# A three-layer fp32 transformer block on one NeuronCore: in two of its three up projections VectorE alone makes the weights' low part

## The chip, the cores and the metric

The kernel runs on one core of one Trainium2 chip. The metric is the device time of one execution in microseconds (us); the number given for a kernel is the median of several executions. The five engines are written as in the profile: PE is TensorE (matmul), PEld its weight loads, DVE VectorE, ACT ScalarE, POOL GpSimd, and SP the engine that issues the DMAs.

## The reference

Three layers over 272 tokens (16 meta tokens and 256 of input) of width 1024. Cut to the part that matters here, each of the first two layers ends in a feed-forward with a causal convolution over tokens:

```python
def conv_ffn(h, w_up, conv_w, conv_b, w_down):
    L = h.shape[1]
    u = h @ w_up                                   # 1024 -> 2 * 2816
    up = jnp.pad(u, ((0, 0), (CONV_WIDTH - 1, 0), (0, 0)))
    u = conv_b + sum(conv_w[j] * up[:, j:j + L] for j in range(CONV_WIDTH))
    gate, val = jnp.split(u, 2, axis=-1)
    return (jax.nn.silu(gate) * val) @ w_down      # 2816 -> 1024
```

Ahead of it stands an attention mixer (layer 0) or a pooling mixer (layer 1). The third layer has a gated linear attention, a feed-forward without the convolution, and a gate with an embedding projection. Every projection is fed by an RMS norm.

## The kernel before

All data are fp32. TensorE multiplies in fp32r, so every operand is held as a high part (rounded to fp32r) and a low part (what the rounding left), and each product is the sum of three matmuls: high by high, low by high and high by low. They are issued by `three`, lines L383 to L385.

**The weight stream.** The weights come in 121 units (`STREAM`, `UNITS`), in the order in which they are used. An up projection (`up0`, `up1`, `up2`) has 22 units of 16 tiles of 128x128; a unit gives one 128-row block of the gate half and one of the value half. A down projection has 8 units of 22 tiles. Unit n goes through slot n % 2 of three double buffers: `raw` (filled by SP, L320), `w_high` (ScalarE, `high`, L783 and L786) and `w_low` (raw minus high: VectorE, `low`, L1116 and L1121, and GpSimd, its own `low`, L1609). Before the change VectorE makes the low part of the first three quarters of the columns (1536 of the 2048 of an up unit) and GpSimd that of the last quarter (512), which is what `vector_cols` says. In the up loops ScalarE and VectorE work in two pieces: the first is `first_half(n)`, half of VectorE's columns rounded to a tile (768), the second is the rest (1280 for ScalarE, 768 for VectorE). GpSimd waits for all of `high`.

**Who waits for whom.** Semaphores count the units that are done: `high_parts`, `low_parts_v`, `low_parts_g`. TensorE waits at the head of a unit for all three (`parts_ready`, L370 to L372). SP waits for all three of unit n - 2 before it loads unit n into the same slot (`slot_free`, L297 to L299). `high(n)` waits for the load and for the matmuls of unit n - 2.

**A turn of an up loop.** `up_turns` writes the 22 turns of each engine: turns 0, 1, 20 and 21 on their own, and turns 2 to 19 in a hardware loop of two turns a pass. Turn j finishes unit j and prepares the weights of unit j + 2, so turns 20 and 21 prepare the first two units of the down projection. In layers 0 and 1 (`conv` true) VectorE's turn is, in this order, which is fixed since each engine runs its instructions one after the other:

- `scaled` twice (L1173): both blocks out of PSUM, times the norm's row, into `conv_in`. This frees the banks.
- `x_full` (L1219): gate times value of the turn before, after ScalarE's silu.
- `low` in two pieces (L1116, L1121). Turn 0 has none; unit 2 is done before the turns.
- four taps of the convolution (L1248) in place on `conv_out`, after ScalarE's tap (L855).
- `x_low` (L1225): the low part of the product of the turn before.

ScalarE's turn is `high` in two pieces (L783, L786), its tap for both halves (L855), `x_high` of the turn before (L836) and, after VectorE's third tap, silu (L862). GpSimd's turn is one instruction (L1609), from the loop in `up_lows`. The third up projection has no convolution and a shorter turn on VectorE.

The first unit of the down projection reads `x_high` and `x_low` of all 22 turns, chunk by chunk, so its last two chunks wait for the end of turns 20 and 21 and for what follows them.

Stages on the time axis of the trace: attention up to about 185 us, `up0` from about 187, `down0` from 321.6, the pooling mixer, `up1` from about 441, `down1` from 572.4, the third layer's mixer, `up2` from about 788 to 908, then `down2` and the rest.

Of the kernel before, what the change touches and what calls it, by code (L numbers as in the profile page):

```python
# [38 lines left out]
ALU = mybir.AluOpType  # L39
# [95 lines left out]


def vector_cols(n):

    return UNITS[n]["tiles"] * P // 3 if UNITS[n]["name"] == "uqn" else (3 * UNITS[n]["tiles"] // 4) * P

# [29 lines left out]
def program(nc, dram, marks, final):  # L170
    ctx = ExitStack()
    with ctx:
# [115 lines left out]
        def _(sp):  # L288
# [5 lines left out]

            def slot_free(n):

                sp.wait_ge(high_parts, n - 1)  # L297
                sp.wait_ge(low_parts_v, n - 1)
                sp.wait_ge(low_parts_g, n - 1)  # L299

            for name, units, tiles, _, _ in STREAM:
                n0, cols, src = FIRST_UNIT[name], tiles * P, dram["w_" + name]
                if units < 8:
                    for u in range(units):
                        n = n0 + u
                        if n == 0:
                            continue
                        if n >= 2:
                            slot_free(n)
                        sp.dma_start(raw[n % 2][:, 0:cols], src[u, :, :]).then_inc(loaded[n % 2], 16)  # L310
                        if n == 1:
                            for dst, src_ in ((ident[:, :], dram["ident"]), (par[:, DC:NPAR], dram["par"][:, DC:NPAR]),
                                              (rope[:, :, :], dram["rope"]), (cmask[:, :], dram["cmask"])):
                                sp.dma_start(dst, src_).then_inc(tables_in, 16)
                else:
                    with sp.Fori(0, units // 2) as i:
                        for k in range(2):
                            n = 2 * i + (n0 + k)
                            slot_free(n)
                            sp.dma_start(raw[(n0 + k) % 2][:, 0:cols], src[2 * i + k, :, :])\  # L320
# [43 lines left out]
        def _(pe):  # L364
            S = Steps("tensor", step_sems["tensor"], marks)

            def parts_ready(n, i=None):
# [3 lines left out]
                pe.wait_ge(low_parts_v, at)  # L371
                pe.wait_ge(low_parts_g, at)  # L372

# [1228 lines left out]
        def _(pool):  # L1602
            S = Steps("pool", step_sems["pool"], marks)

            def low(n, i=None):
# [3 lines left out]
                nc.gpsimd.tensor_tensor(wl[n % 2][:, at], raw[n % 2][:, at], wh[n % 2][:, at].bitcast(F32),  # L1609
                                        ALU.subtract).then_inc(low_parts_g, 1)  # L1610

# [12 lines left out]
            def up_lows(l):  # L1624
                n0 = FIRST_UNIT[f"up{l}"]
                with pool.Fori(0, (FC - 2) // 2) as i:
                    for k in range(2):
                        low(n0 + k + 2, i)
                for j in range(FC - 2, FC):
# [203 lines left out]
```

## Time and profile before

| what | value |
|---|---|
| median of 3 runs | 1013.43 us (1005.52 to 1014.51) |
| the profiled execution | 1012.96 us |
| its span, first to last instruction | 1011.0 us |
| mean granted TensorE clock | 0.955 of full speed |
| busy, share of the span | PE 92%, PEld 89%, DVE 71%, ACT 50%, POOL 39% |
| largest DVE groups (busy us) | L1121 213.9, L1248 87.1, L1116 64.5 |
| all of L1609 on POOL | 121 instructions, 285.4 us |
| q1, the weights' queue | 144.99 MB, 39.9% of 16 engines |

The profiled execution is 0.47 us below the median of the runs, and 1.96 us of it lie outside the span. Busy shares are averages over stages. The end of a matmul is modelled, so the start-to-start spacing of two matmuls says more than the busy time, and the same holds for two neighbouring instructions on VectorE, whose spans overlap by some 0.08 us. A row of the timeline that ends in "x2" or "x4" is two or four instructions merged, with the time from the first start to the last end. "[0.52 <-PE bank L385]" behind a row is the idle time ahead of it and what ended it; a row without it followed at once.

### The profile page before, as it was taken

The numbers are of one execution on the slowest core, as the hardware profiler recorded it, in microseconds if no ns is written. First come the engines' busy times: TensorE is split into PE (matmuls) and PEld (weight loads), VectorE is DVE, ScalarE is ACT, GpSimd is POOL, SyncE is SP. The second block draws the span as 40 slices with busy tenths as digits, with TensorE's granted clock in tenths as the row PEclk, the third lists the DMA queues.
The fourth block names the chain that finished last, engine by engine and source line by source line (L and its number), as shares of the span: only waits on it lengthen the run. The fifth ranks groups of instructions, "written<-read, shape, count | busy, mean of one in ns | idle before, by whom it ended". The sixth has DMA issues, their size and how long they took to land.

```text
span 1011.0 us, 20095 instructions
## 1 busy us (share of the span) xinstructions
PE 934.1 (92%) x7256; PEld 898.8 (89%) x7256; DVE 718.0 (71%) x1224; ACT 504.3 (50%) x833; POOL 397.0 (39%) x274
## 2 busy tenths in 40 slices
PE   6789987999999997899999899899989999999995
PEld 6687777999999897799999899798989999999994
DVE  7656624899999325389999932679868788885666
ACT  5465634555556434555555533453346445454342
POOL 4434736322223455332222356531216333335633
PEclk9799979899999998989999999899999999999997
DMA  7322013244445453024444545334215545455431
GB/s 261 121 84 84 2 42 130 87 168 166 165 165 207 171 192 125 1 88 171 174 172 175 188 165 198 125 124 180 106 52 187 192 173 198 175 210 212 161 125 42
DMA packets 20848, 145.64 MB, mean 144 GB/s; under 512 B 2480, under 2 KB 4032, under 8 KB 5440
## 3 DMA queue, kind: packets, MB, share of 16 engines
q1 hardware_dynamic: 20800, 144.99, 39.9%
q8 instruction: 31, 0.51, 0.2%
q14 instruction: 17, 0.14, 0.0%
HBM read 143.94 MB, written 1.05 MB: 143 GB/s over the span
## 4 chain that ended last, share of the span: by engine, by line
PE 35%; DVE 9%; ACT 5%; issue 5%; ACTq 1%; DVEq 0%; POOL 0%; POOLq 0%
PE bank L383 11%; PE bank L384 10%; PE bank L385 10%; DVE conv_out L1248 3%; ACT w_high L786 2%; DVE w_low L1121 1%; ACT conv_out L855 1%; ACT w_high L783 1%; PE bank L674 1%; PE bank L447 0%; PE bank L702 0%; DVE conv_out L1589 0%; DVE gla_s_diag L1463 0%; PE bank L703 0%; PE bank L704 0%
## 5 line engine op out<-in xcount | busy, mean ns | idle before, releaser
L1609 POOL TENSOR_TENSOR w_low<-raw,w_high 128x512 fp32r<-128x512 f32 (+1 forms) x121 | 285.4, 2359 | 504.7 <-ACT w_high L786 488.5
L383 PE MATMUL bank<-u_high,w_high 128*128 128x256 f32 (+2 forms) x1472 | 432.8, 294 | 30.9 <-DVE u_low L1130 18.8
L384 PE MATMUL bank<-u_low,w_high 128*128 128x256 f32 (+2 forms) x1472 | 425.0, 289 | 0.0
L385 PE MATMUL bank<-u_high,w_low 128*128 128x256 f32 (+2 forms) x1472 | 424.1, 288 | 0.0
L383 PEld LDWEIGHTS bank<-u_high,w_high 128*128 128x128 f32 x1472 | 285.5, 194 | 42.5 <-issue 23.2
L1121 DVE TENSOR_TENSOR w_low<-raw,w_high 128x768 fp32r<-128x768 f32 (+4 forms) x120 | 213.9, 1782 | 142.3 <-ACT w_high L786 141.0
L384 PEld LDWEIGHTS bank<-u_low,w_high 128*128 128x128 f32 x1472 | 285.4, 194 | 0.0
L385 PEld LDWEIGHTS bank<-u_high,w_low 128*128 128x128 f32 x1472 | 284.9, 194 | 0.0
L786 ACT ACTIVATE w_high<-raw 128x1280 fp32r<-128x1280 f32 (+4 forms) x120 | 206.6, 1722 | 70.2 <-PE bank L385 63.8
L383 PE MATMUL bank<-x_high,w_high 128*128 128x256 f32 (+1 forms) x608 | 174.2, 287 | 10.2 <-DVE x_low L1225 4.8
L385 PE MATMUL bank<-x_high,w_low 128*128 128x256 f32 (+1 forms) x608 | 173.7, 286 | 0.0
L384 PE MATMUL bank<-x_low,w_high 128*128 128x256 f32 (+1 forms) x608 | 173.1, 285 | 0.0
L383 PEld LDWEIGHTS bank<-x_high,w_high 128*128 128x128 f32 x608 | 116.0, 191 | 11.6 <-ACT conv_out L862 3.5
L384 PEld LDWEIGHTS bank<-x_low,w_high 128*128 128x128 f32 x608 | 116.0, 191 | 0.0
L385 PEld LDWEIGHTS bank<-x_high,w_low 128*128 128x128 f32 x608 | 115.7, 190 | 0.0
L1622 POOL TENSOR_TENSOR acc<-acc,sq 128x272 f32<-128x272 f32 (+2 forms) x84 | 68.1, 810 | 76.4 <-ACT sq L802 65.1
L1248 DVE SCALAR_TENSOR_TENSOR conv_out<-conv_in,par,conv_out 128x272 f32<-128x272 f32 (+1 forms) x176 | 87.1, 534 | 6.2 <-ACT conv_out L855 0.7
L783 ACT ACTIVATE w_high<-raw 128x768 fp32r<-128x768 f32 (+1 forms) x66 | 56.7, 859 | 60.5 <-PE bank L385 59.8
L862 ACT ACTIVATE conv_out<-conv_out 128x272 f32<-128x272 f32 (+1 forms) x44 | 18.7, 425 | 110.7 <-DVE conv_out L1248 110.7
L1116 DVE TENSOR_TENSOR w_low<-raw,w_high 128x768 fp32r<-128x768 f32 (+1 forms) x66 | 64.5, 977 | 8.6 <-ACT w_high L783 8.6
L1173 DVE TENSOR_TENSOR conv_in<-bank,r_rows 128x256 f32<-128x256 f32 (+2 forms) x140 | 54.1, 427 | 15.7 <-PE bank L385 10.3
L1130 DVE SCALAR_TENSOR_TENSOR u_low<-h,par,u_high 128x272 fp32r<-128x272 f32 (+3 forms) x56 | 53.1, 966 | 0.9 <-ACT u_high L810 0.9
(182 smaller groups left out, 933.3 us busy)
## 6 DMA issues: line engine op xcount, KB each, us to landing
raw<-w_up_dram SPq DMA_DIRECT2D x66, 1024.0 KB, 4.7
raw<-w_down_dram SPq DMA_DIRECT2D x24, 1408.0 KB, 6.0
raw<-w_gin_c_dram SPq DMA_DIRECT2D x4, 1536.0 KB, 7.7
raw<-w_wo_dram SPq DMA_DIRECT2D x4, 1024.0 KB, 4.7
raw<-w_wout_dram SPq DMA_DIRECT2D x4, 1024.0 KB, 4.7
raw<-w_pgate_dram SPq DMA_DIRECT2D x4, 1024.0 KB, 4.8
raw<-w_gin_v_dram SPq DMA_DIRECT2D x2, 1024.0 KB, 4.7
raw<-w_gin_g_dram SPq DMA_DIRECT2D x2, 1024.0 KB, 5.0
```

What stands on the lines that cost most here:

```text
L383: nc.tensor.matmul(out, hi, rhi, start=start, stop=False)
L384: nc.tensor.matmul(out, hi, rlo, start=False, stop=False)
L385: return nc.tensor.matmul(out, lo, rhi, start=False, stop=stop)
L783: nc.scalar.activation(wh[n % 2][:, 0:split], raw[n % 2][:, 0:split], ACT.Copy).then_inc(*S.step(first))
L786: nc.scalar.activation(wh[n % 2][:, split:cols], raw[n % 2][:, split:cols], ACT.Copy).then_inc(high_parts, 1)
L1116: nc.vector.tensor_tensor(wl[n % 2][:, 0:split], raw[n % 2][:, 0:split], wh[n % 2][:, 0:split].bitcast(F32), ALU.subtract).then_inc(*S.step())
L1121: nc.vector.tensor_tensor(wl[n % 2][:, split:cols], raw[n % 2][:, split:cols], wh[n % 2][:, split:cols].bitcast(F32), ALU.subtract).then_i ...
L1130: nc.vector.scalar_tensor_tensor(ul[:, c, 0:T], h[:, c, t0:t0 + T], pcol(gain, c), uh[:, c, 0:T].bitcast(F32), ALU.mult, ALU.subtract)\
L1173: nc.vector.tensor_tensor(out, bank[BLOCKS[b]["bank"]][:, 0:T], rows[:, 0:T], ALU.mult)\
L1248: nc.vector.scalar_tensor_tensor(cv[:, hf, 0:T], ur[:, hf, skip + tap:skip + tap + T], pcol(f"cw{l}", (tap * 2 + hf) * FC + j), cv[:, hf, ...
L1609: nc.gpsimd.tensor_tensor(wl[n % 2][:, at], raw[n % 2][:, at], wh[n % 2][:, at].bitcast(F32), ALU.subtract).then_inc(low_parts_g, 1)
L1622: nc.gpsimd.tensor_tensor(acc[:, a, 0:T], acc[:, a, 0:T], sq[:, label % 2, 0:T], ALU.add).then_inc(*step)
```

## The change

Units 2 to 21 of `up0` and of `up1` (`pool_share` false) are no longer shared: `vector_cols` is all 2048 columns for them, so VectorE makes the whole low part, in pieces of 1024 and 1024. As `first_half` follows, ScalarE's two pieces become 1024 and 1024 too. GpSimd has no instruction for these 40 units; its next `low` (the first unit of `down0` or `down1`) adds 21 to `low_parts_g` in place of 1, so that the counts agree behind it (`pool_counts`). TensorE leaves out its wait for `low_parts_g` at the head of these units, and SP leaves it out where the unit before in the slot was such a unit; for that four units of `up0` and `up1` and two units of each down projection are written out ahead of SP's loops. Units 0 and 1 of `up0` and `up1`, all of `up2`, and all other units are as before, and so are the results: the same subtraction is done by another engine.

```diff
--- before.py
+++ after.py
@@ -134,8 +134,23 @@
     _x["before"] = next((j for j in range(_i - 1, -1, -1) if BLOCKS[j]["bank"] == _x["bank"]), None)
 
 
+def pool_share(n):
+
+    return UNITS[n]["name"] not in ("up0", "up1") or UNITS[n]["u"] < 2
+
+
+def pool_counts(n):
+
+    first = n
+    while first > 0 and not pool_share(first - 1):
+        first -= 1
+    return n - first + 1
+
+
 def vector_cols(n):
 
+    if not pool_share(n):
+        return UNITS[n]["tiles"] * P
     return UNITS[n]["tiles"] * P // 3 if UNITS[n]["name"] == "uqn" else (3 * UNITS[n]["tiles"] // 4) * P
 
 
@@ -292,11 +307,13 @@
                 sp.dma_start(raw[0][:, cols], dram["w_dq"][0, :, cols])\
                     .then_inc(loaded[0] if p == PIECES - 1 else pieces_in[p], 16)
 
-            def slot_free(n):
+            def slot_free(n, shared=True):
+
 
                 sp.wait_ge(high_parts, n - 1)
                 sp.wait_ge(low_parts_v, n - 1)
-                sp.wait_ge(low_parts_g, n - 1)
+                if shared:
+                    sp.wait_ge(low_parts_g, n - 1)
 
             for name, units, tiles, _, _ in STREAM:
                 n0, cols, src = FIRST_UNIT[name], tiles * P, dram["w_" + name]
@@ -306,17 +323,22 @@
                         if n == 0:
                             continue
                         if n >= 2:
-                            slot_free(n)
+                            slot_free(n, pool_share(n - 2))
                         sp.dma_start(raw[n % 2][:, 0:cols], src[u, :, :]).then_inc(loaded[n % 2], 16)
                         if n == 1:
                             for dst, src_ in ((ident[:, :], dram["ident"]), (par[:, DC:NPAR], dram["par"][:, DC:NPAR]),
                                               (rope[:, :, :], dram["rope"]), (cmask[:, :], dram["cmask"])):
                                 sp.dma_start(dst, src_).then_inc(tables_in, 16)
                 else:
-                    with sp.Fori(0, units // 2) as i:
-                        for k in range(2):
+
+                    apart = 2 if units == DC else 4 if not pool_share(n0 + 2) else 0
+                    for u in range(apart):
+                        slot_free(n0 + u, pool_share(n0 + u - 2))
+                        sp.dma_start(raw[(n0 + u) % 2][:, 0:cols], src[u, :, :]).then_inc(loaded[(n0 + u) % 2], 16)
+                    with sp.Fori(0, (units - apart) // 2) as i:
+                        for k in range(apart, apart + 2):
                             n = 2 * i + (n0 + k)
-                            slot_free(n)
+                            slot_free(n, pool_share(n0 + k - 2))
                             sp.dma_start(raw[(n0 + k) % 2][:, 0:cols], src[2 * i + k, :, :])\
                                 .then_inc(loaded[(n0 + k) % 2], 16)
                 if name == "down0":
@@ -369,7 +391,8 @@
                 at = n + 1 if i is None else 2 * i + (n + 1)
                 pe.wait_ge(high_parts, at)
                 pe.wait_ge(low_parts_v, at)
-                pe.wait_ge(low_parts_g, at)
+                if pool_share(n):
+                    pe.wait_ge(low_parts_g, at)
 
             def bank_free(b, i=None, stride=0):
 
@@ -1607,7 +1630,7 @@
                 at = slice(vector_cols(n), UNITS[n]["tiles"] * P)
                 pool.wait_ge(high_parts, n + 1 if i is None else 2 * i + (n + 1))
                 nc.gpsimd.tensor_tensor(wl[n % 2][:, at], raw[n % 2][:, at], wh[n % 2][:, at].bitcast(F32),
-                                        ALU.subtract).then_inc(low_parts_g, 1)
+                                        ALU.subtract).then_inc(low_parts_g, pool_counts(n))
 
             def clear(after, T=T1):
 
@@ -1623,9 +1646,10 @@
 
             def up_lows(l):
                 n0 = FIRST_UNIT[f"up{l}"]
-                with pool.Fori(0, (FC - 2) // 2) as i:
-                    for k in range(2):
-                        low(n0 + k + 2, i)
+                if pool_share(n0 + 2):
+                    with pool.Fori(0, (FC - 2) // 2) as i:
+                        for k in range(2):
+                            low(n0 + k + 2, i)
                 for j in range(FC - 2, FC):
                     low(n0 + j + 2)
```

## Rows read from the trace of the kernel before

**Rows 1.** The page: busy us of each engine (part 1), chain by line (part 4).

```profile
PE 934.1 (92%) x7256; PEld 898.8 (89%) x7256; DVE 718.0 (71%) x1224; ACT 504.3 (50%) x833; POOL 397.0 (39%) x274
...
PE bank L383 11%; PE bank L384 10%; PE bank L385 10%; DVE conv_out L1248 3%; ACT w_high L786 2%; DVE w_low L1121 1%; ACT conv_out L855 1%; ACT w_high L783 1%; PE bank L674 1%; PE bank L447 0%; PE bank L702 0%; DVE conv_out L1589 0%; DVE gla_s_diag L1463 0%; PE bank L703 0%; PE bank L704 0%
```

**Rows 2.** Windows: length, busy us of PE, PEld, DVE, ACT, POOL; granted clock; DMA share; GB/s.

```profile
250.00:260.00 10.00, 9.85 (x77) 9.42 (x76) 9.45 (x19) 5.32 (x9) 1.54 (x1) 1.00 0.45 156
500.00:510.00 10.00, 9.72 (x79) 9.32 (x78) 9.57 (x15) 5.32 (x10) 2.91 (x2) 1.00 0.37 141
583.00:585.00 2.00, 2.00 (x10) 2.00 (x11) 0.00 (x0) 1.09 (x3) 0.55 (x1) 0.50 0.79 327
```

**Rows 3.** VectorE's timeline, one turn of the first up loop: start us, us, what.

```profile
252.95 0.79 DVE L1173 TENSOR_TENSOR conv_in<-bank,r_rows 128x272 f32<-128x272 f32 x2
253.65 0.43 DVE L1219 TENSOR_TENSOR x_full<-conv_out 128x272 f32<-128x272 f32 x1
254.00 0.95 DVE L1116 TENSOR_TENSOR w_low<-raw,w_high 128x768 fp32r<-128x768 f32 x1
254.87 2.04 DVE L1121 TENSOR_TENSOR w_low<-raw,w_high 128x768 fp32r<-128x768 f32 x1
256.84 1.96 DVE L1248 SCALAR_TENSOR_TENSOR conv_out<-conv_in,par,conv_out 128x272 f32<-128x272 f32 x4
258.71 0.43 DVE L1225 TENSOR_TENSOR x_low<-x_full,x_high 128x272 f32 x1
259.27 0.79 DVE L1173 TENSOR_TENSOR conv_in<-bank,r_rows 128x272 f32<-128x272 f32 x2
```

**Rows 4.** GpSimd's timeline, the same turn and one of the third up loop.

```profile
254.56 1.54 POOL L1609 TENSOR_TENSOR w_low<-raw,w_high 128x512 fp32r<-128x512 f32 x1 [4.80 <-ACT w_high L786]
...
825.40 2.06 POOL L1609 TENSOR_TENSOR w_low<-raw,w_high 128x512 fp32r<-128x512 f32 x1 [3.55 <-ACT w_high L786]
```

**Rows 5.** VectorE's timeline, the same turn of the third up loop.

```profile
825.36 0.96 DVE L1121 TENSOR_TENSOR w_low<-raw,w_high 128x768 fp32r<-128x768 f32 x1
826.23 1.51 DVE L1225 TENSOR_TENSOR x_low<-x_full,x_high 128x256 f32 x1
```

**Rows 6.** Groups by line and shape, 315 to 332 us: count, busy us, mean ns.

```profile
L1121 DVE TENSOR_TENSOR w_low<-raw,w_high 128x1024 fp32r<-128x1024 f32 x2 | 2.5, 1226 | 0.0
L1116 DVE TENSOR_TENSOR w_low<-raw,w_high 128x1024 fp32r<-128x1024 f32 x2 | 2.4, 1218 | 0.0
```

**Rows 7.** TensorE's timeline: unit starts of the first up loop, then L383 at 330.78.

```profile
194.52 0.29 PE L383 MATMUL bank<-u_high,w_high 128*128 128x272 f32 x1
...
200.52 0.29 PE L383 MATMUL bank<-u_high,w_high 128*128 128x272 f32 x1
...
257.21 0.39 PE L383 MATMUL bank<-u_high,w_high 128*128 128x272 f32 x1
...
314.26 0.39 PE L383 MATMUL bank<-u_high,w_high 128*128 128x272 f32 x1
...
330.78 0.36 PE L383 MATMUL bank<-x_high,w_high 128*128 128x272 f32 x1 [1.43 <-DVE x_low L1225]
```

**Rows 8.** TensorE's timeline, second up loop: unit starts, and 453.16 inside the first.

```profile
447.72 0.28 PE L383 MATMUL bank<-u_high,w_high 128*128 128x258 f32 x1
...
453.16 0.28 PE L383 MATMUL bank<-u_high,w_high 128*128 128x258 f32 x1
...
509.26 0.39 PE L383 MATMUL bank<-u_high,w_high 128*128 128x258 f32 x1 [0.16 <-issue]
...
565.14 0.38 PE L383 MATMUL bank<-u_high,w_high 128*128 128x258 f32 x1
```

**Rows 9.** VectorE's timeline: start of turn 20 in the first and second up loops.

```profile
316.25 0.79 DVE L1173 TENSOR_TENSOR conv_in<-bank,r_rows 128x272 f32<-128x272 f32 x2
...
567.05 0.76 DVE L1173 TENSOR_TENSOR conv_in<-bank,r_rows 128x258 f32<-128x258 f32 x2
```

**Rows 10.** ScalarE's timeline, the turn of rows 3.

```profile
254.39 1.10 ACT L855 ACTIVATE conv_out<-conv_in,par 128x272 f32<-128x272 f32 x2
```

## The prediction

> **What bounds the kernel now.** I read four views, from the whole to one turn. The page first [rows 1]: VectorE is busy for 71% of the span, and the chain by line is mostly TensorE's three matmul lines with a few per cent of VectorE's taps and of ScalarE's high part. That is an average over stages, so the stage has to be read by itself. The windows of the two up loops [rows 2] show something else there: VectorE is busy for 9.45 and 9.57 us in 10, at full granted clock, and TensorE for 9.85 and 9.72. VectorE is full, and TensorE has small holes.
>
> The timeline of TensorE says how large they are. In the first up loop a unit of 48 matmuls took 200.52 - 194.52 = 6.00 us at the start, with nothing between the two unit heads. Later the heads stand at 257.21 and 314.26, nine units apart: 6.34 us each [rows 7]. In the second loop (258 tokens wide in place of 272) 15 chunks of three matmuls took 453.16 - 447.72 = 5.44 us, so 16 of them, a unit, take 5.80. From 509.26 to 565.14 nine units took 6.21 each [rows 8]. So TensorE loses 0.34 us a unit in one loop and 0.41 in the other.
>
> Who makes it wait stands in VectorE's timeline [rows 3]. One turn runs from 252.95 to 259.27, 6.32 us, and no row has an idle time: VectorE is the bound of the loop. Start to start, its steps take 0.70 (conv_in), 0.35 (x_full), 0.87 (first low piece), 1.97 (second low piece), 1.87 (taps) and 0.56 us (x_low and the way to the next turn). The second low piece ends at 254.87 + 2.04 = 256.91 and TensorE's next unit starts at 257.21: this is the wait that ends last at the head of a unit.
>
> The two low pieces have the same shape, 128x768, and cost 0.95 and 2.04 us. What differs is that GpSimd's instruction started 0.31 us ahead of the second one [rows 4]. The third up loop is the control: there GpSimd started at 825.40, just after VectorE's second piece at 825.36. That piece took 0.96, and the next VectorE instruction, x_low, took 1.51, where x_low takes 0.43 in the turn of the first loop [rows 3 to 5]. So 1.1 us of VectorE's time is lost once per unit, in whichever two-input instruction meets GpSimd's, and it does not belong to the low piece.
>
> The Trainium skill has this in SBUF — State Buffer, section "Who interferes with whom": a VectorE instruction with two inputs in SBUF and a GpSimd instruction that reads SBUF exclude each other, and the one that came first keeps the port. By that rule, the trace agrees in who waits; the length lost, 2.04 - 0.95, is less than GpSimd's whole 1.54, which is also how the rows overlap.
>
> **The change, part by part.** VectorE's low part. For 40 units the pieces grow from 768 to 1024 columns. That shape is in the trace, in turns 20 and 21: 1.22 and 1.23 us [rows 6], against 0.95. Start to start that is the duration less the usual overlap of 0.08, so about 1.15 each, 2.30 together, where rows 3 have 0.87 + 1.97 = 2.84. Two larger pieces add 2 x 0.27 = 0.54, the lost 1.09 goes, and VectorE's turn gets 0.54 shorter: 6.32 - 0.54 = 5.78 us in the first loop and 6.21 - 0.54 = 5.67 in the second. Both are below TensorE's 6.00 and 5.80, so TensorE becomes the bound, and of the 0.54 only 0.34 and 0.41 count.
>
> ScalarE. Its pieces of 768 and 1280 become 1024 and 1024. The sum of columns is the same. The first piece comes some 0.2 us later (1.04 in place of 0.84), the second ends at the same time. In the turn of rows 3 ScalarE's taps ended at 254.39 + 1.10 = 255.49 [rows 10] and VectorE's taps began at 256.84, so ScalarE is 1.35 us ahead; with VectorE 0.54 faster it stays ahead. I price it at nothing inside the loop. When VectorE has caught up with TensorE, its first piece will wait some 0.1 to 0.3 us for ScalarE's first piece, an estimate. The cover is the 0.13 to 0.22 us between VectorE's turn and TensorE's unit; where that is gone, TensorE still isn't late, since it needs the low part only a whole unit later (5.8 us against about 3.6).
>
> GpSimd, the waits and the loads. GpSimd's 40 instructions go, and nothing else is queued in its loop. TensorE has one wait fewer per unit, SP likewise, and SP's load is released by VectorE's second piece, which now ends sooner. Issues and sizes are the same, only some are written out ahead of the loop. Nothing.
>
> The start of each loop. Unit 2's low part is made ahead of turn 0, without GpSimd beside it, so VectorE pays 0.54 there and again in turn 1. The 1.1 us lost to GpSimd in turn 1 goes at the same time, so VectorE enters turn 2 about where it did. What TensorE could wait there is at most the 0.54 us by which the first banks come free later, once a loop. I take zero, since TensorE's unit 2 follows unit 1 without a hole now, and keep 0.5 for the range.
>
> Units 2 to 21. In the first loop the head of unit 2 is at 194.52, and 19 units later the head of unit 21 would be at 194.52 + 19 x 6.00 = 308.52, where it is 314.26 now [rows 7]: 5.7 us. In the second 447.72 + 19 x 5.80 = 557.92 against 565.14 [rows 8]: 7.2 us. Together 12.9.
>
> The end of each loop is not TensorE's. At 330.78 it waits for x_low of VectorE's turn 20 [rows 7], and once more for turn 21. Turns 20 and 21 keep GpSimd's share and their length, so this end moves with the start of VectorE's turn 20. Now that start is at 316.25 and 567.05, which is 1.99 and 1.91 us behind the head of unit 21 [rows 7 to 9], since VectorE is late all through the loop. With TensorE as the bound VectorE makes up 0.22 us a turn in the first loop, 4.0 us over 18 turns, and in the second 0.13 a turn, 2.3 us; both are more than the 2.0 and 1.9. So turn 20 starts close behind unit 20's end, and I take 0.1 to 0.2: 308.6 and 558.1. The ends move by 316.25 - 308.6 = 7.65 and 567.05 - 558.1 = 8.95. From each I take 0.15 for the first low piece of turn 20, which now waits a little for ScalarE: 7.5 + 8.8 = 16.3 us. Behind it the down projection runs on TensorE's time, so the gain is kept.
>
> Sum against the profiled execution: 1012.96 - 16.3 = 996.7. The median of the runs is 0.47 above that execution, hence 997.
>
> One term I can't place: TensorE's clock. Behind the two waits at the end of the second loop it fell to half (0.50 from 583 to 585 [rows 2]), 1.3 us or so lost over 2.7 us. The new waits there will be some 0.3 us shorter in sum. The fall may go, or one may come behind the first loop, where there is none now: 1.3 either way.
>
> **The rivals.** The tail gives nothing. If VectorE doesn't catch up (its turn is 5.9 rather than 5.7, by waits that are now hidden), only the 12.9 us of TensorE's unit heads are won: 1000.5. For it: in the second loop the margin is only 0.13 us a turn. Against: no idle row in VectorE's turn [rows 3].
>
> ScalarE's chain is the bound. The chain of the page has its high part and VectorE's taps in it [rows 1], which reads like a circle silu, high, tap, taps. If it set the turn, VectorE's shorter low part would only become idle time, and the time would stay at 1013. Against: the 1.35 us between ScalarE's tap and VectorE's [rows 3, 10], which VectorE's second low piece fills.
>
> Slower: the 1.1 us is a cost of the second piece itself (it runs beside ScalarE's taps), not of GpSimd. Then the new second piece takes 1.22 + 1.10 = 2.32, the two pieces some 3.38 start to start, and a turn grows by 0.54: 40 turns, +21.6 us, 1034. It decides from the point where the two pieces take more than today's 2.84. Against: the piece of 0.96 in rows 5, and the two of rows 6. The Trainium skill, Perfetto Trace Analysis, section "Optimizing Scalar/DVE Operations", speaks on both sides: with VectorE saturated some of its work may be worth giving to another engine, GpSimd included, but between these two it might not help, for their common port. The first half of that is what the change undoes; the trace agrees with the second half, by the 1.1 us lost against the 0.54 that the columns cost.
>
> **How the numbers follow.** 997 has 0.70, with a range of its own from 993 to 1000 (the clock 1.3 either way, the start 0.5, 0.05 us a turn on 40 turns for TensorE's rate, 2). The tail giving nothing has 0.13, ScalarE's chain 0.09 and the slower case 0.05; 0.03 is for what I don't see. The three runs of before lie 9 us apart, so a median can fall some 4 us beside the profile. To hold 8 in 10 I take 989 to 1004: the first case with that spread, and the second one. Faster by over 1% (below 1003.3; 1% is about what a measurement of this kernel can tell from no change) is the first two cases less the spread: 0.79. Within 1%: 0.15. Slower by over 1%: 0.06.
>
> **What would show it.** In the changed profile both low pieces should be 1.22 us at 128x1024 in all 40 turns. TensorE's unit heads should stand 6.00 and 5.80 us apart without a hole. VectorE should have short idle times in late turns that end at TensorE or at ScalarE's first high piece. Turn 20 should start near 308.6, and in the second loop near 550.6 (558.1 less the first loop's 7.5). GpSimd should be empty in the loops. A second piece above 1.3 us, or unit heads further apart than 6.05 and 5.85, would prove me wrong.

## The result, and the profile after

| kernel | median of its runs | beside it, before |
|---|---|---|
| changed | 994.67 us (992.07 to 996.30, 4 runs) | 1010.70 us (1005.52 to 1014.51, 4 runs) |
| changed, a second set | 994.65 us (991.24 to 996.17, 5 runs) | 1011.39 us (1009.33 to 1013.54, 9 runs) |

The ratio to the kernel before is 0.9838, 95% interval 0.9807 to 0.9868, and in the second set 0.9835, 0.9811 to 0.9858. The profiled executions took 1012.96 and 996.30 us, 16.66 less; 16.3 was predicted, and 997 for the median. That the median came out 2.3 us below 997 has little to do with the change: the prediction started from a median of 1013.43 us for the kernel before (3 runs), and beside the changed kernel it is 1010.70, which less 16.3 is 994.4.

Line numbers of the changed kernel are 23 higher in the part shown: L383 to L385 are L406 to L408, L1116 and L1121 are L1139 and L1144, L1609 is L1632.

The windows of the changed kernel, with the columns of [rows 2] and at the same times (the third is one window of 2 us behind the second loop's end):

```profile
250.00:260.00 10.00, 10.00 (x82) 10.00 (x81) 9.32 (x16) 6.35 (x11) 0.00 (x0) 1.00 0.42 151
500.00:510.00 10.00, 10.00 (x85) 10.00 (x85) 9.45 (x17) 6.44 (x11) 0.00 (x0) 1.00 0.47 168
568.00:570.00 2.00, 2.00 (x17) 2.00 (x18) 0.00 (x0) 1.32 (x3) 0.74 (x1) 1.00 0.84 349
```

TensorE is busy for 10.00 us in 10, where it was 9.85 and 9.72. VectorE is a little under its old value, and GpSimd is empty. TensorE's granted clock behind the second loop is 1.00, the upper of its two levels (2.4 GHz), where it was 0.50, the lower one (1.2 GHz).

VectorE's timeline of the changed kernel, one turn late in the first loop:

```profile
285.07 0.79 DVE L1196 TENSOR_TENSOR conv_in<-bank,r_rows 128x272 f32<-128x272 f32 x2
285.78 0.43 DVE L1242 TENSOR_TENSOR x_full<-conv_out 128x272 f32<-128x272 f32 x1
286.33 1.23 DVE L1139 TENSOR_TENSOR w_low<-raw,w_high 128x1024 fp32r<-128x1024 f32 x1
287.48 1.22 DVE L1144 TENSOR_TENSOR w_low<-raw,w_high 128x1024 fp32r<-128x1024 f32 x1
288.62 1.97 DVE L1271 SCALAR_TENSOR_TENSOR conv_out<-conv_in,par,conv_out 128x272 f32<-128x272 f32 x4
290.50 0.43 DVE L1248 TENSOR_TENSOR x_low<-x_full,x_high 128x272 f32 x1
291.06 0.79 DVE L1196 TENSOR_TENSOR conv_in<-bank,r_rows 128x272 f32<-128x272 f32 x2
```

ScalarE's timeline of the changed kernel, its first high piece of the same turn:

```profile
285.24 1.06 ACT L806 ACTIVATE w_high<-raw 128x1024 fp32r<-128x1024 f32 x1 [0.60 <-PE bank L408]
```

Against [rows 3]: the pieces cost 1.23 and 1.22 us in place of 0.95 and 2.04, and all 88 pieces of this shape in the two stages took 1.22 or 1.23. The turn is 5.99 us long, TensorE's length, and a first slack shows: 0.55 us from x_full to the first low piece, where it was 0.35. VectorE waits there for ScalarE, whose high piece ends at 286.30, and ScalarE waited for TensorE (the 0.60 in its row). This is the order of a loop that TensorE bounds.

TensorE's timeline of the changed kernel: head of unit 2 and of unit 21 of the second loop, then the first matmul of chunk 20 in layer 0's first down unit:

```profile
441.22 0.28 PE L406 MATMUL bank<-u_high,w_high 128*128 128x258 f32 x1
...
551.42 0.28 PE L406 MATMUL bank<-u_high,w_high 128*128 128x258 f32 x1
...
324.29 0.37 PE L406 MATMUL bank<-x_high,w_high 128*128 128x272 f32 x1 [1.32 <-DVE x_low L1248]
```

(551.42 - 441.22) / 19 = 5.80 us a unit, where [rows 8] have 6.21. In the first loop the heads of units 2 and 21 stand at 195.04 and 309.04, 19 units of 6.00 us apart, and no matmul of either loop between these heads has an idle time ahead of it.

**Where the 16.7 us went.** Two marks bound each loop's stage: the matmul in the middle of unit 1 that waits for the norm's rows, and the first matmul of chunk 21 in the first down unit, which waits for VectorE's turn 21. All stage lengths below are differences of two such starts on TensorE's timeline.

| stage, us | before | changed | difference |
|---|---|---|---|
| start to first mark | 191.42 | 191.94 | +0.52 |
| first loop and tail | 140.85 | 133.83 | -7.02 |
| between the loops | 112.47 | 112.47 | 0.00 |
| second loop and tail | 138.13 | 129.73 | -8.40 |
| chunk 21 of down1 to the next norm's matmul at 639.74 and 623.33 | 56.87 | 55.36 | -1.51 |

The loops give 15.4 us. The 1.5 us behind the second loop is the clock: it was at half from 583 to 585 and in part up to 587, and now isn't. The other profiles bear this out: the stretch of the last row takes 56.70 to 56.88 us in the four that have this fall (before, e1, e3, e9) and 55.21 to 55.42 in the eight that don't. The rest of the kernel is as it was to within 0.1 us. The sum is 7.0 + 8.4 + 1.5 + 0.1 - 0.5 = 16.5 us of the span; the other 0.2 of the 16.66 lie outside the span.

These stage lengths are much sharper than whole times. The mark in unit 1 of the first loop stood between 186.33 and 191.94 us in the profiles of this study. Nothing that the kernels change lies ahead of it but a memset of GpSimd's at the start of e8 and e9 and, in the norm just before it, GpSimd's low part of unit 2. The granted clock differs there: 0.87 from 20 to 60 us and 0.91 from 60 to 100 in the kernel before, 0.83 and 1.00 in e5. That is not the whole of it, for e3 had the clock of before up to 100 us, a lower one behind it (0.84 against 0.86 from 100 to 186), and its mark all the same 0.84 us earlier. Behind that mark stages that should be equal agree to 0.02 us. So the experiments are read by their stages, and by their medians only where those are far apart.

### The profile page after: what moved, and what is told of

It reads as the page before. It is cut to its first block, busy times and chain, and to the rows that moved or that the text cites. A ratio compares the mean times of both kernels' runs of the same rounds, so it can differ in the third digit from the quotient of the medians.

```text
span 994.5 us, 19919 instructions
## 1 busy us (share of the span) xinstructions
PE 923.7 (93%) x7256; PEld 895.8 (90%) x7256; DVE 698.3 (70%) x1224; ACT 506.6 (51%) x833; POOL 335.0 (34%) x234
## 3 DMA queue, kind: packets, MB, share of 16 engines
HBM read 143.94 MB, written 1.05 MB: 146 GB/s over the span
## 4 chain that ended last, share of the span: by engine, by line
PE 78%; DVE 12%; ACT 5%; issue 2%; POOL 1%; DMA 1%; SPq 0%; POOLq 0%; DVEq 0%; ACTq 0%
PE bank L406 22%; PE bank L407 22%; PE bank L408 22%; DVE w_low L1144 2%; PE bank L580 2%; ACT w_high L809 2%; PE bank L566 2%; DVE conv_out L1271 1%; PE bank L697 1%; PE bank L596 1%; DVE u_low L1153 1%; PE bank L667 1%; PE bank L470 1%; PE bank L455 1%; PE bank L460 1%
## 5 line engine op out<-in xcount | busy, mean ns | idle before, releaser
L406 PE MATMUL bank<-u_high,w_high 128*128 128x256 f32 (+2 forms) x1472 | 429.1, 292 | 27.1 <-DVE u_low L1153 17.9
L408 PE MATMUL bank<-u_high,w_low 128*128 128x256 f32 (+2 forms) x1472 | 424.2, 288 | 0.0
L1632 POOL TENSOR_TENSOR w_low<-raw,w_high 128x512 fp32r<-128x512 f32 (+1 forms) x81 | 223.8, 2764 | 551.4 <-ACT w_high L809 535.1
L406 PEld LDWEIGHTS bank<-u_high,w_high 128*128 128x128 f32 x1472 | 286.1, 194 | 31.4 <-issue 13.0
L1144 DVE TENSOR_TENSOR w_low<-raw,w_high 128x1024 fp32r<-128x1024 f32 (+4 forms) x120 | 186.0, 1550 | 142.3 <-ACT w_high L809 141.1
L408 PEld LDWEIGHTS bank<-u_high,w_low 128*128 128x128 f32 x1472 | 285.3, 194 | 0.0
L809 ACT ACTIVATE w_high<-raw 128x1024 fp32r<-128x1024 f32 (+5 forms) x120 | 197.9, 1650 | 70.3 <-PE bank L408 63.7
L406 PE MATMUL bank<-x_high,w_high 128*128 128x256 f32 (+1 forms) x608 | 173.5, 285 | 7.9 <-DVE x_low L1248 4.7
L408 PE MATMUL bank<-x_high,w_low 128*128 128x256 f32 (+1 forms) x608 | 173.0, 285 | 0.0
L406 PEld LDWEIGHTS bank<-x_high,w_high 128*128 128x128 f32 x608 | 115.2, 190 | 9.3 <-ACT conv_out L885 3.3
L408 PEld LDWEIGHTS bank<-x_high,w_low 128*128 128x128 f32 x608 | 115.0, 189 | 0.0
L806 ACT ACTIVATE w_high<-raw 128x1024 fp32r<-128x1024 f32 (+1 forms) x66 | 65.7, 995 | 77.6 <-PE bank L408 77.5
L1139 DVE TENSOR_TENSOR w_low<-raw,w_high 128x1024 fp32r<-128x1024 f32 (+1 forms) x66 | 75.5, 1143 | 11.9 <-ACT w_high L806 9.1
L825 ACT ACTIVATE sq<-bank 128x272 f32<-128x272 f32 (+1 forms) x24 | 9.4, 394 | 86.8 <-PE bank L408 86.8
```

The lines of the kernel that those rows point to most:

```text
L406: nc.tensor.matmul(out, hi, rhi, start=start, stop=False)
L408: return nc.tensor.matmul(out, lo, rhi, start=False, stop=stop)
L806: nc.scalar.activation(wh[n % 2][:, 0:split], raw[n % 2][:, 0:split], ACT.Copy).then_inc(*S.step(first))
L809: nc.scalar.activation(wh[n % 2][:, split:cols], raw[n % 2][:, split:cols], ACT.Copy).then_inc(high_parts, 1)
L1139: nc.vector.tensor_tensor(wl[n % 2][:, 0:split], raw[n % 2][:, 0:split], wh[n % 2][:, 0:split].bitcast(F32), ALU.subtract).then_inc(*S.step())
L1144: nc.vector.tensor_tensor(wl[n % 2][:, split:cols], raw[n % 2][:, split:cols], wh[n % 2][:, split:cols].bitcast(F32), ALU.subtract).then_i ...
```

## The experiments

Each is told as an edit of the changed kernel unless it says otherwise.

**e1: GpSimd reads, and nobody waits for it.**

```diff
+        scratch = sb("scratch", [P, 512])
...
                 if pool_share(n0 + 2):
                     ...
+                else:
+                    for j in range(FC - 2):
+                        pool.wait_ge(high_parts, n0 + j + 3)
+                        pool.wait_ge(*S.now())
+                        nc.gpsimd.tensor_tensor(scratch[:, 0:NPAR], par[:, 0:NPAR], par[:, 0:NPAR],
+                                                ALU.subtract).then_inc(*S.step())
```

> The changed kernel, and beside it GpSimd subtracts a table of 476 columns from itself into a scratch tile once in each of the 40 turns, at the moment where its low part ran before (after ScalarE's high part); nobody waits for it. Theory (GpSimd's instruction that reads SBUF holds up VectorE's instruction with two inputs): VectorE loses about 1.0 us a turn (476 of 512 columns of 1.1), its turn goes from 5.78 and 5.67 to 6.8 and 6.7 us and is the bound again; TensorE's unit heads stand 6.8 and 6.7 apart in place of 6.00 and 5.80; some +32 to +36 us, 1027 to 1031. Rival (the 1.1 us belonged to VectorE's second low piece, or to the wait for the low part): nobody waits for the added work, so 995 as the changed kernel.

Measured: 1019.76 us (1018.58 to 1021.44, 4 runs), ratio to before 1.009 (1.006 to 1.0121), 25 us above the changed kernel. By stages 145.20 and 142.58, that is +11.4 and +12.9. VectorE's timeline of e1, and GpSimd's instruction:

```profile
251.06 0.79 DVE L1197 TENSOR_TENSOR conv_in<-bank,r_rows 128x272 f32<-128x272 f32 x2
251.76 0.43 DVE L1243 TENSOR_TENSOR x_full<-conv_out 128x272 f32<-128x272 f32 x1
252.11 1.22 DVE L1140 TENSOR_TENSOR w_low<-raw,w_high 128x1024 fp32r<-128x1024 f32 x1
253.25 2.00 DVE L1145 TENSOR_TENSOR w_low<-raw,w_high 128x1024 fp32r<-128x1024 f32 x1
...
257.60 0.79 DVE L1197 TENSOR_TENSOR conv_in<-bank,r_rows 128x272 f32<-128x272 f32 x2
...
252.66 1.50 POOL L1658 TENSOR_TENSOR scratch<-par 128x476 f32<-128x476 f32 x1 [5.07 <-ACT w_high L810]
```

The mechanism is shown: an instruction whose result nobody reads brings the slow second piece back, and with it a turn of 6.54 us in place of 5.99. The rival (995) falls. The size was short of what I expected, 0.78 us lost in place of 1.0, and a turn of 6.54 in place of 6.8; e8 takes that up. The total holds some 3 us that are not the turns': in e1 the granted clock fell to 0.50 behind both loops (from 333 to 336 us and from 589 to 592), which made the stretches behind them 1.8 and 1.3 us longer than in the changed kernel.

**e2: GpSimd only writes.** As e1, with the instruction replaced:

```diff
-  nc.gpsimd.tensor_tensor(scratch[:, 0:NPAR], par[:, 0:NPAR], par[:, 0:NPAR], ALU.subtract)
+  nc.gpsimd.memset(scratch[:, 0:512], 0.0)
```

> As e1, but GpSimd's added instruction only writes: a memset of 512 columns (272 columns took 0.33 us in the profile, so this takes some 0.5). Theory (what is shared is the way by which GpSimd reads): no change, 995, VectorE's pieces stay at 1.22 us. Rival (any GpSimd instruction holds VectorE up for its length): 0.5 us a turn, VectorE's turn 6.3 and 6.2, +12 to +16 us, about 1009.

Measured: 991.89 us (991.43 to 993.44, 4 runs), ratio 0.9815 (0.9787 to 0.9844); stages 133.83 and 129.72, the changed kernel's to 0.01 us.

VectorE's second piece in the timeline of e2, and GpSimd's memset of the same turn:

```profile
252.77 1.22 DVE L1145 TENSOR_TENSOR w_low<-raw,w_high 128x1024 fp32r<-128x1024 f32 x1
...
252.59 0.53 POOL L1658 MEMSET scratch<- 128x512 f32 x1 [5.47 <-ACT w_high L810]
```

The memset runs across the start of the second piece, as the reading instruction did, and the piece keeps its 1.22 us. The rival (1009) falls. So it is not GpSimd's being busy, and not its writing, but its reading. The Trainium skill says just this in SBUF — State Buffer, section "Who interferes with whom": a VectorE instruction with two SBUF inputs contends with a GpSimd instruction that reads SBUF and not with one that only writes. By that rule, e1 and e2 agree.

**e8: two tables in place of one twice.** As e1, with a second table of the same width that GpSimd fills at the start:

```diff
-  nc.gpsimd.tensor_tensor(scratch[:, 0:NPAR], par[:, 0:NPAR], par[:, 0:NPAR], ALU.subtract)
+  nc.gpsimd.tensor_tensor(scratch[:, 0:NPAR], par[:, 0:NPAR], table2[:, 0:NPAR], ALU.subtract)
```

> As e1, but GpSimd's added subtraction reads two different tables of 476 columns in place of one table twice. In e1 VectorE's second piece lost 0.78 us (2.00 in place of 1.22), where 512 columns of the real low part cost 1.09. If reading one table twice is what made e1 cheap, the loss is 1.0 and VectorE's turn 6.8 us in the first loop; if it is where GpSimd begins in VectorE's turn (0.59 us ahead of the second piece in e1, 0.31 in the kernel before), it is 0.78 and 6.54 again.

One run: 1022.90 us. The timeline of e8, the same instructions as in e1:

```profile
252.44 0.79 DVE L1198 TENSOR_TENSOR conv_in<-bank,r_rows 128x272 f32<-128x272 f32 x2
...
253.50 1.22 DVE L1141 TENSOR_TENSOR w_low<-raw,w_high 128x1024 fp32r<-128x1024 f32 x1
254.63 2.23 DVE L1146 TENSOR_TENSOR w_low<-raw,w_high 128x1024 fp32r<-128x1024 f32 x1
...
254.06 1.73 POOL L1659 TENSOR_TENSOR scratch<-par,table 128x476 f32<-128x476 f32 x1 [5.08 <-ACT w_high L811]
```

The second piece took 2.23 to 2.25 us over the turns, a loss of 1.02 on average, and the turn 6.78 (from 252.44 to 259.22). The stages are 149.96 and 147.33, +33.7 us on the changed kernel in sum, inside what e1 had been expected to cost; the whole time is less far up, since the first mark stands 5.6 us earlier than in the changed kernel's first profile. GpSimd begins 0.57 us ahead of the second piece, as in e1 (0.59), so its place in the turn is not the reason. A subtraction of one table from itself holds VectorE up for less than one of two tables, 0.78 against 1.02 us at the same 476 columns. Why, no run here shows.

**e9: one input.** As e8, with

```diff
+  nc.gpsimd.tensor_scalar(scratch[:, 0:512], table2[:, 0:512], 1.5, None, ALU.mult)
```

> As e1, but GpSimd's added instruction is a tensor_scalar of 512 columns with one SBUF input. Theory (every GpSimd instruction that reads SBUF keeps VectorE's two-input instruction waiting, for about as long as it runs beside it): VectorE loses 0.4 to 1.0 us a turn. Rival (only GpSimd's two-input instructions do): nothing, VectorE's pieces stay at 1.22 and the unit heads at 6.00 us.

One run: 1003.95 us; stages 137.86 and 135.23, +4.0 and +5.5.

The timeline of e9, VectorE's two pieces and GpSimd's instruction of the same turn:

```profile
254.26 1.22 DVE L1141 TENSOR_TENSOR w_low<-raw,w_high 128x1024 fp32r<-128x1024 f32 x1
255.40 1.63 DVE L1146 TENSOR_TENSOR w_low<-raw,w_high 128x1024 fp32r<-128x1024 f32 x1
...
254.77 2.06 POOL L1659 TENSOR_SCALAR scratch<-table 128x512 f32<-128x512 f32 x1 [4.12 <-ACT w_high L811]
```

It loses VectorE 0.41 us, at the low end of the expectation, and the rival (nothing) falls. GpSimd's record is 2.06 us long and runs for 1.43 us beside VectorE's second piece, which still loses only 0.41. So the theory's "for about as long as it runs beside it" fails for an instruction with one input.

**e7: GpSimd's share doubled, on the kernel before.**

```diff
 def vector_cols(n):
 
+    if UNITS[n]["name"] in ("up0", "up1") and UNITS[n]["u"] >= 2:
+        return 8 * P
```

> The kernel before with GpSimd's share of the 40 units raised from 512 to 1024 columns; VectorE's pieces fall to 512 and 512. Theory (VectorE loses time in proportion to GpSimd's columns): the loss goes from 1.1 to about 2.2 us and VectorE wins 0.54, so its turn grows by 0.56 us, 6.9 and 6.8; about +22 us on the kernel before, 1032. Rival (the loss is a fixed 1.1 us for each instruction that meets): VectorE's turn falls by 0.54 to 5.8 and 5.7, TensorE is the bound, 995.

Measured: 1031.92 us (1030.66 to 1037.24, 4 runs), ratio 1.0222 (1.019 to 1.0253); stages 151.59 and 149.15, +21.8 us in sum on the kernel before.

The timeline of e7, the same three instructions:

```profile
255.24 0.68 DVE L1118 TENSOR_TENSOR w_low<-raw,w_high 128x512 fp32r<-128x512 f32 x1
255.84 2.90 DVE L1123 TENSOR_TENSOR w_low<-raw,w_high 128x512 fp32r<-128x512 f32 x1
...
255.80 2.40 POOL L1611 TENSOR_TENSOR w_low<-raw,w_high 128x1024 fp32r<-128x1024 f32 x1 [4.54 <-ACT w_high L788]
```

Two pieces of the same 512 columns, 0.68 and 2.90 us: 2.22 lost for 1024 of GpSimd's columns, 1.09 for 512 before. That is 2.1 to 2.2 ns a column, and VectorE does a column itself in (1.22 - 0.95) / 256 = 1.05 ns. So in these VectorE-bound stages each column that is given to GpSimd costs VectorE twice what it saves. The fixed price falls. In nine turns of the second loop GpSimd's record begins a little later, within the second piece, and the loss falls on the taps: the second piece takes 0.69 us, and the four taps 3.93 to 4.04, where they take some 1.9 without GpSimd. It is the next instruction with two inputs that pays, whichever it is.

**What VectorE waits for.** In all these runs GpSimd's record begins while an instruction of VectorE is still running. Set against the end of that instruction, the numbers fall into line. Means over the turns of both loops in which the second low piece was hit, us:

| run, GpSimd's instruction | its record | its part behind VectorE's first piece | lost by the second piece |
|---|---|---|---|
| before, 512 columns, two inputs | 1.34 to 1.61 | 1.15 | 1.10 |
| e7, 1024 columns, two inputs | 2.39 to 2.46 | 2.27 | 2.22 |
| e1, 476 columns, one table twice | 1.07 to 1.58 | 0.84 | 0.78 |
| e8, 476 columns, two tables | 1.31 to 1.81 | 1.07 | 1.02 |
| e9, 512 columns, one input | 1.80 to 2.08 | 1.35 | 0.41 |

GpSimd's record varies by up to 0.5 us within one kernel, and the part behind the first piece doesn't. That fits a GpSimd that waits for VectorE's first piece, with the wait inside its record, and then holds VectorE's second piece up to its own end, in the four cases with two inputs. In [rows 5] it is the same: GpSimd's record ends at 827.46, 1.14 us behind VectorE's piece (826.32), and x_low loses 1.1. With one input (e9) the second piece loses far less than GpSimd's part behind the first; why, no run here shows.

**e3: the first loop alone.**

```diff
-    return UNITS[n]["name"] not in ("up0", "up1") or UNITS[n]["u"] < 2
+    return UNITS[n]["name"] not in ("up0",) or UNITS[n]["u"] < 2
```

> The change in the first up loop alone; the second keeps GpSimd's share. Theory (each loop gives its own part): 7.0 us of the gain stay and 8.4 and perhaps the 1.5 us of clock go, so 1003 to 1005. Rival (one loop carries the gain, by the clock or by where the loads fall): 995 or 1011.

Measured: 1003.82 us (1001.43 to 1005.38, 4 runs), ratio 0.992 (0.989 to 0.9951); stages 133.83 and 138.11. The first is the changed kernel's, the second the one of before (138.13). The loops don't touch each other, and both rivals (995, 1011) fall. The fall of the clock behind the second loop is back too (0.52 from 575 to 578).

**e4: VectorE's turn shorter still.**

```diff
     if not pool_share(n):
-        return UNITS[n]["tiles"] * P
+        return (3 * UNITS[n]["tiles"] // 4) * P
```

> The 40 units' low part is made by VectorE for 1536 columns as before the change, in pieces of 768, and by nobody for the last 512, where old data stay: that part of the computation is left out. VectorE's turn is 1.1 us shorter than before the change and 0.54 shorter than after it, 5.24 and 5.13 us. Theory (after the change TensorE is the bound of the loop, by 6.00 and 5.80 us): the same time as the changed kernel within 1 us, 994 to 996, and unit heads at 6.00 and 5.80. Rival (VectorE still sets part of the turn): up to 20 us less, 975 to 985.

Measured: 992.97 us (991.50 to 996.65, 4 runs), ratio 0.9832 (0.9796 to 0.9867); stages 133.83 and 129.71, equal to the changed kernel's. VectorE's timeline of e4:

```profile
250.74 0.82 DVE L1196 TENSOR_TENSOR conv_in<-bank,r_rows 128x272 f32<-128x272 f32 x2 [0.38 <-PE bank L408]
```

All that VectorE saves turns into waiting for TensorE, and the rival falls. So 0.34 and 0.41 us a unit was all that the turns inside the loops had to give, and nothing done to VectorE can give more there. ScalarE's pieces are 768 and 1280 again in this run, as before the change, so the new split of its work isn't what gained the time either.

**e6: the third up loop too.**

```diff
-    return UNITS[n]["name"] not in ("up0", "up1") or UNITS[n]["u"] < 2
+    return UNITS[n]["name"] not in ("up0", "up1", "up2") or UNITS[n]["u"] < 2
```

> As the changed kernel, and units 2 to 21 of up2 too. There VectorE's turn has idle time (0.5 us ahead of conv_in, 0.45 ahead of the first low piece, in a turn of 5.61 us) and TensorE runs without holes at 5.61 us a unit. Theory (the change pays only where VectorE is the bound): no change within 1 us, 995. Rival (GpSimd's share costs wherever it stands): 0.54 us in 20 turns, 984.

Measured: 993.16 us (990.76 to 994.66, 5 runs) against 994.65 (991.24 to 996.17, 5 runs) for the changed kernel in the same set. From chunk 21 of down1 to the end of the span, which holds the third loop, it took 992.7 - 566.15 = 426.55 us, and the changed kernel 994.5 - 567.97 = 426.53. The rival (984) falls. VectorE's wait ahead of conv_in, 0.52 us in the kernel before, is 1.01 here, in its timeline of e6:

```profile
821.20 0.78 DVE L1196 TENSOR_TENSOR conv_in<-bank,r_rows 128x256 f32<-128x256 f32 x2 [1.01 <-PE bank L408]
```

The same contention, removed in the same way, is worth nothing where TensorE is the bound.

**e5: the first two down units too.** They are made in turns 20 and 21.

```diff
 def pool_share(n):
 
+    if UNITS[n]["name"] in ("down0", "down1"):
+        return UNITS[n]["u"] >= 2
...
+        count_up = sb("count_up", [P, 1])
...
-                    apart = 2 if units == DC else 4 if not pool_share(n0 + 2) else 0
+                    apart = (2 if pool_share(n0) else 4) if units == DC else 4 if not pool_share(n0 + 2) else 0
...
-                                        ALU.subtract).then_inc(low_parts_g, pool_counts(n))
+                                        ALU.subtract).then_inc(low_parts_g, 1)
...
                 for j in range(FC - 2, FC):
-                    low(n0 + j + 2)
+                    if pool_share(n0 + j + 2):
+                        low(n0 + j + 2)
+                if not pool_share(n0 + FC):
+                    nc.gpsimd.memset(count_up[:, :], 0.0).then_inc(low_parts_g, FC)
```

> As the changed kernel, and GpSimd also leaves the first two units of down0 and of down1 to VectorE (2816 columns in pieces of 1408), which are made in turns 20 and 21 of the up loops. There GpSimd's 768 columns now hold VectorE's taps up by 1.5 us a turn (3.44 us for four taps, against 1.97) and VectorE would pay 0.8 us for the columns. Theory (the end of each loop is VectorE's): 0.7 us a turn, four turns, about 3 us less than the changed kernel, 992. Rival (ScalarE's high pieces set turns 20 and 21): nothing, 995; or the fall of the clock comes back with other waits, up to 1.5 us more.

Measured: 987.07 us (986.97 to 991.66, 5 runs), ratio to before 0.9783 (0.9758 to 0.9809), beside 0.9835 (0.9811 to 0.9858) for the changed kernel in the same set. Stages 132.32 and 127.86, -1.51 and -1.87; behind the second loop it is 0.8 shorter again (425.79 against 426.56 in the changed kernel of that set). This 0.8 can't be put down to the edit: in the changed kernel of that set the clock was at 0.50 from 703 to 706 us, in the third layer's mixer, e5 has no such fall there, and the stretch between the norms on either side is 0.9 shorter. e8, which leaves the down units as they are, lacks the same fall. Turn 20 of the changed kernel, then that of e5, on VectorE:

```profile
308.97 0.79 DVE L1196 TENSOR_TENSOR conv_in<-bank,r_rows 128x272 f32<-128x272 f32 x2
...
310.39 1.23 DVE L1139 TENSOR_TENSOR w_low<-raw,w_high 128x1024 fp32r<-128x1024 f32 x1 [0.29 <-ACT w_high L806]
311.99 1.23 DVE L1144 TENSOR_TENSOR w_low<-raw,w_high 128x1024 fp32r<-128x1024 f32 x1 [0.37 <-ACT w_high L809]
313.13 3.44 DVE L1271 SCALAR_TENSOR_TENSOR conv_out<-conv_in,par,conv_out 128x272 f32<-128x272 f32 x4
...
316.96 0.79 DVE L1196 TENSOR_TENSOR conv_in<-bank,r_rows 128x272 f32<-128x272 f32 x2
```

```profile
303.75 0.79 DVE L1199 TENSOR_TENSOR conv_in<-bank,r_rows 128x272 f32<-128x272 f32 x2
...
305.51 1.63 DVE L1142 TENSOR_TENSOR w_low<-raw,w_high 128x1408 fp32r<-128x1408 f32 x1 [0.62 <-ACT w_high L809]
307.06 1.62 DVE L1147 TENSOR_TENSOR w_low<-raw,w_high 128x1408 fp32r<-128x1408 f32 x1
308.59 1.86 DVE L1274 SCALAR_TENSOR_TENSOR conv_out<-conv_in,par,conv_out 128x272 f32<-128x272 f32 x4
...
310.84 0.79 DVE L1199 TENSOR_TENSOR conv_in<-bank,r_rows 128x272 f32<-128x272 f32 x2
```

The four taps fall from 3.44 to 1.86 us, the pieces grow from 1.23 to 1.63, and the turn goes from 7.99 to 7.09. The expected 3 us came to 3.4 in the two stages. The medians are 7.6 apart, but 2.6 us of the profiles' difference lies ahead of the first mark (186.49 against 189.10), where the kernels are the same. So e5 beats both kernels, the changed one by 3.4 us by its stages. The rival, that ScalarE sets these turns, falls as the whole; its part is the 0.62 us.

**The changed kernel again**, beside e5 to e7:

> The changed kernel once more, beside the runs of this set: 995 within 2 us.

It took 994.65 us (991.24 to 996.17, 5 runs), with stages of 133.83 and 129.73 us, those of its first profile.

## Why the prediction was right, point by point

**VectorE as the bound of the loops, and the wait at the unit head.** Right: with its turn shorter by 0.54 us the holes at TensorE are gone, and e1 brings the long turn back with nothing but one more instruction on GpSimd, for which nobody waits.

**The 1.1 us belong to GpSimd's reading.** Argued from the control in the third loop [rows 4, 5], and shown by e1 against e2. The slower rival, a cost of the second piece itself, is refuted by the changed kernel (1.22 us) and by e1. The prediction left open why the loss (1.09) is shorter than GpSimd's record (1.54): the record holds GpSimd's own wait for VectorE's first piece, as the table behind e7 suggests.

**The price of the columns and the new turn.** Right: 1.23 and 1.22 us, and in early turns, where VectorE still runs behind, conv_in to conv_in is 207.44 - 201.67 = 5.77 us against the 5.78 of the sum. The wait for ScalarE's first piece, put at 0.1 to 0.3 us once VectorE has caught up, is 0.55 - 0.35 = 0.20.

**TensorE's rates.** 6.00 and 5.80 us, as predicted to the hundredth. These terms, 5.7 + 7.2 us, carry most of the result, and e4 shows that they are all that the turns inside the loops hold.

**The tail.** The place was right and its size was a little off in two ways that partly cancel. VectorE's turn 20 starts at 308.97 and 551.47. Set to the time axis of before (0.52 us at the first mark, 444.74 - 438.24 = 6.50 at the second), it starts 7.80 and 9.08 us earlier than in [rows 9], where 7.65 and 8.95 were predicted. But then the turn is longer: 316.96 - 308.97 = 7.99 and 559.26 - 551.47 = 7.79 us, against 7.20 and 7.12 before. The term that was too small is the 0.15 us taken off for ScalarE: it measured 0.79 and 0.67. Start to start, the first low piece came 0.37 and 0.30 us later in the turn than before, and the second one another 0.42 and 0.36. I had priced the wait for the first piece only, and at less than half. ScalarE's second piece of a down unit, 1792 columns in 1.69 us, is late as well, since with VectorE on time the whole of ScalarE's chain starts at the end of TensorE's unit. Hence 7.0 + 8.4 in place of 7.5 + 8.8.

**The clock.** The term that I couldn't place went the good way: 1.5 us, where 1.3 either way was kept open. So the total came out at 16.7 partly by luck: one term was 0.9 too large, one of 1.5 the sum didn't hold, and 0.5 was lost ahead of the first mark. That the fall had to go is not shown. The waits behind the second loop, from which I argued, were to get 0.3 us shorter; the one for chunk 20 was 1.97 us and is 1.93, the one for chunk 21 is as it was. The row of chunk 20 has 1.65 to 1.69 us of idle time ahead of it in every profile but e5's, and yet the fall is there in before, e1, e3 and e9 only. It is not there in e7 and e8, where VectorE bounds the second loop too. A fall behind the first loop, which I had thought possible, came in e1 and e9. What decides it stays open.

**A part that I left out.** GpSimd's low part of unit 2 also fell into VectorE's norm ahead of turn 0, and one instruction of 0.16 us took 1.20 there. So the longer low part in front of turn 0 was more than paid for there already, and not only in turn 1. It made no difference to the time, as TensorE was in the middle of unit 1.

**The rivals.** The tail giving nothing: refuted, since the stages gave 1.3 and 1.2 us more than the unit heads' 5.7 and 7.2. ScalarE's chain as the bound: refuted in the loop, and partly true of turns 20 and 21.

## What to carry to other kernels

An engine that has time to spare is no free help when its reading holds up the one that is full: here 2.2 ns a column were lost where 1.05 were saved. Compare the same instruction with and without the helper beside it, and count what it loses against what it would pay to do the work itself. Then look at which engine bounds the stage, for that alone says whether the answer is worth anything: the same edit gave 7.0, 8.4 and 0.0 us in three loops. Behind such a gain the end of the loop, where the turns differ, is the next place to look.

## What the runs showed of the hardware that I had not expected

- GpSimd's record is not all time that VectorE loses. With two inputs the loss was the part of the record behind the VectorE instruction that was running when it began, less 0.05 or 0.06 us: 1.10 us of a record of 1.34 to 1.61 for 512 columns, 2.22 of 2.39 to 2.46 for 1024. With one input (e9) it was 0.41 us, of a part of 1.35.
- The loss is 2.1 to 2.2 ns for each of GpSimd's columns with two inputs. The Trainium skill, GPSIMD Engine Reference, section "Elementwise — side-by-side cycle accounting", has about 2.6 cycles an element for its tensor_tensor and puts that down to the reading of two inputs through one port; at the 1.2 GHz given there that is 2.17 ns, an estimate from that page. The rate of loss measured here agrees with it; that VectorE's loss is GpSimd's time for reading is not shown by it.
- Reading one table twice cost VectorE 0.78 us and two tables 1.02 at the same width (e1, e8).
- The first loop's stage was 133.83 us in six profiles (changed twice, e2, e3, e4, e6) and the second's 129.71 to 129.73 in five of them, while whole times of one kernel spread over 2 to 9 us. Between the two profiles of the changed kernel 2.8 of the 3.1 us lay ahead of the first mark.
- A fall of the granted clock to 0.50 behind the second loop cost 1.3 to 1.5 us, and came in four profiles of twelve.
